# Turning the first layer's cached key pages in 32x32 blocks on VectorE, with the pages fetched by quarters of their width

## The chip, the cores and the metric

One core of one Trainium2 chip runs the whole program. The metric is the device time in microseconds (us) of one execution. The numbers of the trace come from one profiled execution, taken by the hardware profiler.

## The reference

Two layers of a hybrid decoder run as one step for two groups of requests: a prompt of 512 positions, and 8 samples of 8 new positions each that have 1024 cached positions behind them. The change is in the attention of layer 0, which has 8 forgetting ("fox") heads and 4 differential heads. For a sample it reads 8 cached pages of keys and 8 of values, each page 128 positions by 1024 floats:

```python
def fox_diff_attend(qa, qb, cq, q_pos, ka, va, ck, kb, vb, k_pos, lam, subln0):
    sa = jnp.einsum('bqhd,bkhd->bhqk', qa, ka).astype(jnp.float32) * scale
    sa = sa + (jnp.swapaxes(cq, 1, 2)[..., :, None] - jnp.swapaxes(ck, 1, 2)[..., None, :])
    pa = jax.nn.softmax(jnp.where(causal, sa, -jnp.inf), axis=-1)
    oa = jnp.einsum('bhqk,bkhd->bqhd', pa.astype(va.dtype), va)
    sb = jnp.einsum('bqhcd,bkhcd->bhcqk', qb, kb).astype(jnp.float32) * scale
    pb = jax.nn.softmax(jnp.where(causal, sb, -jnp.inf), axis=-1)
    diff = pb[:, :, 0] - lam * pb[:, :, 1]
    ob = jnp.einsum('bhqk,bkhe->bqhe', diff.astype(vb.dtype), vb)
...
        k_all = jnp.concatenate([cache_k[pt].reshape(past, L0_KV_WIDTH), k_b], axis=0)
        v_all = jnp.concatenate([cache_v[pt].reshape(past, L0_KV_WIDTH), v_b], axis=0)
```

The scores sum over the width of a key (the 64 columns of a head). TensorE sums over partitions, and a page lands with its positions on the partitions, so each key page has to be turned before it can be scored.

## The kernel before, in words

The class `FirstAttention` does the attention of layer 0 for the prompt and the samples in one stage. Its five methods `tensor`, `scalar`, `gpsimd`, `vector` and `sync` write out the order of TensorE (PE), ScalarE (ACT), GpSimd (POOL), VectorE (DVE) and SyncE (SP) by hand, with semaphores between them.

The stage has 32 slots. Slot x does one unit of the prompt, a pair of heads with one of the four query blocks of 128 rows: `PAIR_ORDER` takes the four differential pairs first (16 "mixed" units, whose two maps of probabilities are blended into one), then the four fox pairs. The query blocks come in the order 2, 1, 3, 0, so that a unit's width is 384, 256, 512 or 128 columns. Beside the prompt, slots 4b to 4b+3 (k = 0 to 3) carry sample b: its 8 key pages are turned, two in each slot, and scored from k = 1 on; the softmax comes at k = 0 of the next sample; its 8 value pages are weighed in the slots after that.

- **Loads.** SP issues one DMA for each page (`load_key` L1907, `load_value` L1912), of [128 partitions x 1024], 512 KB in rows of 4 KB. The page's number is first read into a register of SP (`value_load`, L1902), from which the address is worked out. There are 5 places for key pages, 4 for value pages and 3 for turned pages. A load into a used place waits until the page in it has been turned (`turned_b`) or weighed (`value_used`). Keys run 5 pages ahead. By the order of SP's loop, 52 of the 64 value pages are issued ahead of the last key page.
- **Turning.** `turn_keys` (L1468) makes 8 transposes of 128x128 for each page on PE (L1474), four into each of two PSUM banks (`RING`). ACT copies one bank to the turned page (`keys_out` L1621, copy at L1618), DVE the other (`keys_out` L1745, copy at L1749).
- **Scoring and weighing.** `score_page` (L1487, matmuls L1483) and `weigh_page` (L1521, matmuls L1531) use 32-wide tiles of PE; the prompt's scores, the transposes and the prompt's `weigh` use 128-wide or 64-wide tiles. A slot's order on PE is: scores, turn a page, weigh a page, turn the probabilities of unit x-1, score a page, turn a page, weigh a page, score a page, `weigh(x-1)`.
- **DVE** in a slot: the blend of unit x-1, the row maxima of unit x (`top`, L1762), one key copy, the second another, then the sums of unit x (L1767, L1771), and the samples' softmax pieces.

Of the kernel before, what the change touches and what calls it, by code (L numbers as in the profile page):

```python
# [18 lines left out]
P = 128  # L19
# [49 lines left out]
def constant_table():  # L69
# [13 lines left out]
    row_head, row_query = i // DEC_SEQ, i % DEC_SEQ  # L83
# [4 lines left out]
    put("selections", selections)  # L88
    put("new_mask", np.where(h8[None, :] <= row_query[:, None], 0.0, NEG))
# [1246 lines left out]
class FirstAttention:  # L1336
# [7 lines left out]
    def __init__(self, nc, K, mem, qp, kp, vp, qs, ks, vnew, retired, next_tile):  # L1344
# [3 lines left out]
                 "turned_a", "turned_b", "emptied_a", "emptied_b", "chain", "pool_chain",  # L1348
# [12 lines left out]
        self.knew, self.snew, self.st = sb("knew", [P, KC, DEC_SEQ]), sb("snew", [P, DEC_SEQ]), sb("st", [P, 2, 10])  # L1361
        self.squares = sb("squares", [P, DIFF, SEQ])
# [18 lines left out]
        self.fills_after_key = {}  # L1381
        self.fill_of_second_probs = {}
        self.fill_of_second_head = {}
# [21 lines left out]
    def tensor(self, pe):  # L1405
        K, S = self.K, self.S
        filled = [0, 0]
        turned, emptied = (S["turned_a"], S["turned_b"]), (S["emptied_a"], S["emptied_b"])

        def ring(x):  # L1410
            if filled[x]:
                pe.wait_ge(emptied[x], filled[x])
            filled[x] += 1
            return self.RING[x]
# [16 lines left out]
        def turn(u):  # L1431
            p, qt = self.units[u]
            for i in range(1 if self.mixed(u) else 2):
                bank = ring(i)
                if self.mixed(u):
                    pe.wait_ge(S["blended"], self.count(u + 1, True))
                for j in range(qt + 1):
                    ins = pe.transpose(bank[:, j * P:(j + 1) * P], self.probs[:, u % 2, i, j * P:(j + 1) * P], K.c("ident"))
                ins.then_inc(turned[i], 1)
                if i:  # L1440
                    self.fill_of_second_head[u] = filled[1]
            self.head_fills = (filled[0], filled[1])

        def weigh(u):
            p, qt = self.units[u]
            pe.wait_ge(emptied[0], self.head_fills[0])
            if not self.mixed(u):
                pe.wait_ge(emptied[1], self.head_fills[1])
# [1830 lines left out]
```

## Time and profile before

| | us |
|---|---|
| three runs | 1892.20, 1894.41, 1894.65 |
| median | 1894.41 |
| the profiled execution's own time | 1891.96 |
| its span, first to last instruction | 1890.2 |

The mean granted TensorE clock over the span is 0.957 of full. Over the span PE is busy 1707.6 us (90%), DVE 853.5 (45%), ACT 603.2 (32%) and POOL 151.1 (8%). The stage of the change runs from the first scores at 226.9 us to the first matmul of the next stage at 521.2 us.

How to read it: busy shares are means over stages that have different limits. Matmuls are pipelined, so that the time of a group of them is best read from one start to the next. DMA issues stand on the queue of the engine that issues them (SPq is SP's), and the time beside an issue is what SP spends on it; the transfer follows behind it. A DMA share near 1 says that the core's 16 DMA engines are all occupied.

### The profile page before, as it was taken

Reading aid. Unit: us, or ns where it says so; the run is one execution under the profiler, and the core shown is the slowest. Engines: PE = TensorE matmul, PEld = TensorE weight load, DVE = VectorE, ACT = ScalarE, POOL = GpSimd, SP = SyncE. Lnnn points to the kernel's source line nnn. Section 1 sums busy time; section 2 is a strip of 40 time slices with the busy share of each in tenths; the row PEclk is TensorE's granted clock in tenths of the full one; section 3 lists DMA queues with packets and bytes.
Section 4 is the critical chain, followed back from the end, with each engine's and each line's share of the span. In section 5 each row is a group of like instructions: output and inputs, shape, how many; then the busy total and the mean of one; then the engine's idle time right before and its main releaser. Section 6 shows DMA issues by size and latency. Waiting matters only on the chain. (4 is left out here: it accounts for less than half of the span.)

```text
span 1890.2 us, 32284 instructions
## 1 busy us (share of the span) xinstructions
PE 1707.6 (90%) x12454; PEld 1422.2 (75%) x12462; DVE 853.5 (45%) x1570; ACT 603.2 (32%) x1275; POOL 151.1 (8%) x303
## 2 busy tenths in 40 slices
PE   5999788998798999999998788687888999999998
PEld 3787565665478999799987576355457999889987
DVE  4446455445435322323224978985545232233323
ACT  3325344433223321112213344554333232112220
POOL 1222223111000000000000012110000000000000
PEclk9999899999898999999998899798999999999999
DMA  5232278766632222333321112101752322233221
GB/s 183 68 117 57 86 265 278 269 218 222 205 101 67 76 79 84 87 104 83 105 76 59 48 45 48 46 1 47 217 137 67 89 68 83 84 90 85 70 84 67
DMA packets 177043, 201.61 MB, mean 107 GB/s; under 512 B 21650, under 2 KB 131538, under 8 KB 176914
## 3 DMA queue, kind: packets, MB, share of 16 engines
q1 hardware_dynamic: 167634, 189.39, 32.6%
q10 hardware_dynamic: 9200, 10.24, 1.7%
q8 instruction: 81, 1.33, 0.3%
q14 instruction: 48, 0.39, 0.1%
q0 software_dynamic: 80, 0.26, 0.1%
HBM read 190.77 MB, written 9.08 MB: 106 GB/s over the span
## 5 line engine op out<-in xcount | busy, mean ns | idle before, releaser
L211 PE MATMUL ps<-feat_lo,w_hi 128*128 128x288 f32 x1408 | 416.5, 296 | 7.4 <-PEq L2451 3.8
L213 PE MATMUL ps<-feat_hi,w_hi 128*128 128x288 f32 x1408 | 416.5, 296 | 0.0
L212 PE MATMUL ps<-feat_hi,w_lo 128*128 128x288 f32 x1408 | 416.1, 296 | 0.0
L193 DVE TENSOR_TENSOR w_lo<-w_raw,w_hi 128x2048 fp32r<-128x2048 f32 x96 | 220.1, 2292 | 339.5 <-ACT w_hi L187 339.4
L187 ACT ACTIVATE w_hi<-w_raw 128x2048 fp32r<-128x2048 f32 x96 | 183.6, 1913 | 348.8 <-PE ps L219 334.9
L211 PEld LDWEIGHTS ps<-feat_lo,w_hi 128*128 128x128 f32 x1408 | 265.7, 189 | 8.6 <-issue 4.4
L212 PEld LDWEIGHTS ps<-feat_hi,w_lo 128*128 128x128 f32 x1408 | 265.7, 189 | 0.0
L213 PEld LDWEIGHTS ps<-feat_hi,w_hi 128*128 128x128 f32 x1408 | 265.5, 189 | 0.0
L2551 DVE TENSOR_TENSOR f_prod<-f_silu,ps 128x576 f32<-128x576 f32 x44 | 33.2, 754 | 361.1 <-ACT f_silu L2530 361.1
L211 PE MATMUL ps<-w_lo,feat_hi 128*128 128x512 f32 (+1 forms) x448 | 182.4, 407 | 13.5 <-DVE feat_lo L2403 5.5
L212 PE MATMUL ps<-w_hi,feat_lo 128*128 128x512 f32 (+1 forms) x448 | 177.9, 397 | 0.0
L213 PE MATMUL ps<-w_hi,feat_hi 128*128 128x512 f32 (+1 forms) x448 | 177.8, 397 | 0.0
L2530 ACT ACTIVATE f_silu<-ps 128x576 f32<-128x576 f32 x44 | 28.7, 652 | 429.6 <-PE ps L213 429.6
L212 PE MATMUL ps<-w_hi,f_act_lo 128*128 128x512 f32 x352 | 137.0, 389 | 0.0
L211 PE MATMUL ps<-w_lo,f_act_hi 128*128 128x512 f32 x352 | 137.0, 389 | 0.0
L213 PE MATMUL ps<-w_hi,f_act_hi 128*128 128x512 f32 x352 | 136.9, 389 | 0.0
L211 PEld LDWEIGHTS ps<-w_lo,feat_hi 128*128 128x128 f32 x448 | 88.6, 198 | 32.3 <-issue 14.4
L213 PEld LDWEIGHTS ps<-w_hi,feat_hi 128*128 128x128 f32 x448 | 87.9, 196 | 17.9
L212 PEld LDWEIGHTS ps<-w_hi,feat_lo 128*128 128x128 f32 x448 | 88.6, 198 | 16.1
L1474 PE MATMUL ps<-const,places 128*128 128x128 f32 x512 | 70.7, 283 | 13.4 <-ACT a_probs_t L1618 8.6
L213 PEld LDWEIGHTS ps<-w_hi,f_act_hi 128*128 128x128 f32 x352 | 66.1, 188 | 13.7
L211 PEld LDWEIGHTS ps<-w_lo,f_act_hi 128*128 128x128 f32 x352 | 66.1, 188 | 13.6
(340 smaller groups left out, 2386.4 us busy)
## 6 DMA issues: line engine op xcount, KB each, us to landing
places<-in_cache_l_k_dram SPq DMA_DIRECT2D x64, 512.0 KB, 4.5
places<-in_cache_l_v_dram SPq DMA_DIRECT2D x64, 512.0 KB, 5.1
w_raw<-in_w_gate_dram SPq DMA_DIRECT2D x44, 512.0 KB, 4.0
w_raw<-in_w_up_dram SPq DMA_DIRECT2D x44, 512.0 KB, 5.3
w_raw<-in_w_in_dram SPq DMA_DIRECT2D x18, 1024.0 KB, 5.2
w_raw<-in_w_down_dram SPq DMA_DIRECT2D x16, 1024.0 KB, 5.1
s_kslot<-in_cache_l_k_dram SPq DMA_DIRECT2D x56, 128.0 KB, 2.8
w_raw<-in_w_down_dram SPq DMA_DIRECT2D x8, 768.0 KB, 4.3
```

The lines of the kernel that those rows point to most:

```text
L187: act.activation(self.K.w_hi[:, n % 2, :], self.K.w_raw[:, n % 2, :], ACT.Copy).then_inc(self.split_hi, 1)
L193: dve.tensor_tensor(self.K.w_lo[:, n % 2, :], self.K.w_raw[:, n % 2, :], self.K.w_hi[:, n % 2, :].bitcast(F32), ALU.subtract).then_inc(sel ...
L211: pe.matmul(out, lhs[0], rhs[1], start=start, stop=False)
L212: pe.matmul(out, lhs[1], rhs[0], start=False, stop=False)
L213: return pe.matmul(out, lhs[0], rhs[0], start=False, stop=stop)
L1474: ins = pe.transpose(bank[:, c * P:(c + 1) * P], self.keys[g % self.KEY_PLACES][:, at:at + P], K.c("ident"))
L2530: act.activation(silu[:, x, :, :], K.ps[:, 4 * x:4 * x + 2, 0:H], ACT.Silu).then_inc(S["silu_ok"], 1)
L2551: dve.tensor_tensor(prod[:, x, :, :], silu[:, x, :, :], K.ps[:, 4 * x + 2:4 * x + 4, 0:H], ALU.mult)\
```

## The change

A key page is no longer turned by PE. SP fetches it by quarters of its width: four DMAs for each page, quarter a (256 columns) into partitions 32a to 32a+31, each of those partitions holding four runs of 256 columns, 1 KB each. So the block structure of the turned page is made by the DMAs, and what is left is a transpose of each 32x32 block, which one VectorE instruction does for the whole page from SBUF to SBUF. The order of the rows of a turned page is another one than before; the queries (`q_rows`), the samples' new keys (`k_rows`), the table `selections`, and the copies out of the samples' probabilities are reordered to suit, and a small matmul by the constant `swap` reorders the softmax factor.

```diff
@@ FirstAttention.tensor
-        def turn_keys(g):
-            pe.wait_ge(self.k_in[g % self.KEY_PLACES], 16 * (g // self.KEY_PLACES + 1))
-            for x in range(2):
-                bank = ring(x)
-                for c in range(4):
-                    at = (4 * x + c) * P
-                    ins = pe.transpose(bank[:, c * P:(c + 1) * P], self.keys[g % self.KEY_PLACES][:, at:at + P], K.c("ident"))
-                ins.then_inc(turned[x], 1)
...
-            pe.wait_ge(emptied[0], self.key_fills[g][0])
-            pe.wait_ge(emptied[1], self.key_fills[g][1])
+            pe.wait_ge(S["keys_turned"], g + 1)
...
         for x in range(self.SLOTS + 1):
             b, k = divmod(x, 4)
-            if k == 1 and b >= 2:
+            if k == 1 and b:
+                turn_new_probs(b - 1)
+                swap_factor(b - 1)
+            if k == 2 and b >= 2:
                 turn_o(b - 2)
             if x < self.SLOTS:
                 scores(x)
-                turn_keys(2 * x)
+            if x:
+                turn(x - 1)
...
             if before >= 0:
                 weigh_page(before, first)
-            if x:
-                turn(x - 1)
-            if x < self.SLOTS and k:
-                score_page(b, 2 * k - 2)
-            if x < self.SLOTS:
-                turn_keys(2 * x + 1)
-            if before >= 0:
                 weigh_page(before, first + 1)
...
             if x < self.SLOTS and k:
+                score_page(b, 2 * k - 2)
                 score_page(b, 2 * k - 1)
@@ FirstAttention.scalar
-        def keys_out(g):
-            if g >= self.TURNED_PLACES:
-                act.wait_ge(S["page_scored"], g - self.TURNED_PLACES + 1)
-            empty(self.turned[g % self.TURNED_PLACES][:, 0:4, :], self.RING[0].rearrange("p (c n) -> p c n", n=P))
...
         def head_out(u):
-            if u >= 2:
-                act.wait_ge(S["weighed"], u - 1)
-            empty(self.probs_t[:, u % 2, 0, 0:self.width(u)], self.RING[0][:, 0:self.width(u)])
+            for i in range(1 if self.mixed(u) else 2):
+                if i == 0 and u >= 2:
+                    act.wait_ge(S["weighed"], u - 1)
+                empty(self.probs_t[:, u % 2, i, 0:self.width(u)], self.RING[i][:, 0:self.width(u)])
...
+        def probs_out(b):
+            nonlocal emptied
+            for half in range(2):
+                dst = self.pt[:, 4 * half:4 * half + 4, :].rearrange("p j (x y q) -> p y (j x) q", x=4, y=4)
+                src = self.RING[half].rearrange("p (j y x q) -> p y j x q", j=4, y=4, x=4)
+                emptied += 1
+                act.wait_ge(S["act_turned"], emptied)
+                for y in range(4):
+                    ins = act.activation(dst[:, y].rearrange("p (j x) q -> p j x q", j=4), src[:, y], ACT.Copy)
+                ins.then_inc(S["act_emptied"], 1)
@@ FirstAttention.vector
-        def keys_out(g):
+        def turn_keys(g):
+            dve.wait_ge(self.k_in[g % self.KEY_PLACES], 64 * (g // self.KEY_PLACES + 1))
             if g >= self.TURNED_PLACES:
                 dve.wait_ge(S["page_scored"], g - self.TURNED_PLACES + 1)
-            bank = filled()
-            dve.tensor_copy(self.turned[g % self.TURNED_PLACES][:, 4:8, :], bank.rearrange("p (c n) -> p c n", n=P))\
-               .then_inc(S["emptied_b"], 1)
+            src = self.keys[g % self.KEY_PLACES].rearrange("p (g c n) -> p g c n", g=4, c=KC)
+            dst = self.turned[g % self.TURNED_PLACES].rearrange("p c (g n) -> p g c n", g=4)
+            dve.transpose(dst, src).then_inc(S["keys_turned"], 1)
@@ FirstAttention.sync
         def load_key(g):
             if g >= self.KEY_PLACES:
-                sp.wait_ge(S["turned_b"], self.fills_after_key[g - self.KEY_PLACES])
-            sp.dma_start(self.keys[g % self.KEY_PLACES], page(K.cache_l0_k, g)).then_inc(self.k_in[g % self.KEY_PLACES], 16)
+                sp.wait_ge(S["keys_turned"], g - self.KEY_PLACES + 1)
+            src = page(K.cache_l0_k, g).rearrange("(g k) (a n) -> a k g n", g=4, a=4)
+            dst = self.keys[g % self.KEY_PLACES].rearrange("p (g n) -> p g n", g=4)
+            for a in range(4):
+                sp.dma_start(dst[32 * a:32 * a + 32], src[a]).then_inc(self.k_in[g % self.KEY_PLACES], 16)
```

Besides, GpSimd copies a sample's queries with 4 instructions instead of 16, ACT empties the banks that held both halves of the samples' probabilities, and DVE no longer copies a second head of probabilities.

The order of SP, one key page and one value page, with what it waits for. Before (`places` are the key and value buffers; `a0_turned_b` says that a key page has left its place):

```order
L1902 TENSOR_LOAD pages [waits a0_turned_b]
L1902 ISA x2
L1910 ISA
L1910 DMA places<-in_cache_l_k_dram 128x1024
L1902 TENSOR_LOAD pages [waits a0_value_used]
L1902 ISA x2
L1922 ISA
L1922 DMA places<-in_cache_l_v_dram 128x1024
```

After, one key page:

```order
L1921 TENSOR_LOAD pages [waits a0_keys_turned]
L1921 ISA x2
L1932 ISA
L1932 DMA places<-in_cache_l_k_dram 32x4x256
L1932 ISA
L1932 DMA places<-in_cache_l_k_dram 32x4x256
L1932 ISA
L1932 DMA places<-in_cache_l_k_dram 32x4x256
L1932 ISA
L1932 DMA places<-in_cache_l_k_dram 32x4x256
```

The address instruction and the DMA stand four times behind one page number, and the DMA has 32 partitions of 4 runs of 256 elements. The value page keeps its form.

The order of PE in one slot of the mixed units (the third slot of a sample, of width 512). Before:

```order
L1423 MATMUL ps<-kp,qp 128x512 x2
L1428 MATMUL ps<-causal_bf,ident_bf 128x128 x2
L1474 MATMUL ps<-const,places 128x128 x8
L1531 MATMUL ps<-places,free_49 32x256 x4
L1438 MATMUL ps<-const,a_probs 128x128 x2
L1483 MATMUL ps<-places,free_49 32x128 x8
L1474 MATMUL ps<-const,places 128x128 x8
L1531 MATMUL ps<-places,free_49 32x256 x4
L1483 MATMUL ps<-places,free_49 32x128 x8
L1464 MATMUL ps<-a_probs_t,vp 128x128 x2
```

After:

```order
L1424 MATMUL ps<-kp,qp 128x512 x2
L1429 MATMUL ps<-causal_bf,ident_bf 128x128 x2
L1441 MATMUL ps<-const,a_probs 128x128 x2
L1528 MATMUL ps<-places,free_49 32x256 x8
L1471 MATMUL ps<-places,free_49 32x128 x16
L1463 MATMUL ps<-a_probs_t,vp 128x128 x2
```

The 16 transposes of key pages are gone, the turn of the probabilities stands right behind the scores, and the two weighings and the two scorings stand together.

The order of DVE in the same kind of slot, with what it waits for. Before:

```order
L1762 TENSOR_REDUCE a_minus<-ps 128x2 [waits a0_scored]
L1749 COPY places<-ps 128x512 [waits a0_turned_b,a0_page_scored] x2
L1767 RECIPROCAL a_scale<-a_total 128x2 [waits a0_exped]
L1771 TENSOR_SCALAR a_scale<-a_scale,minus_lam 128x1 [waits a0_summed]
L1777 SCALAR_TENSOR_TENSOR a_probs<-a_probs,a_scale 128x256 [waits a0_chain,a0_scaled]
```

After:

```order
L1783 TENSOR_REDUCE a_minus<-ps 128x2 [waits a0_scored]
L1779 STREAM_TRANSPOSE places<-places 128x4x8x32 [waits a0_page_scored,a0_k_in_0]
L1779 STREAM_TRANSPOSE places<-places 128x4x8x32 [waits a0_page_scored,a0_k_in_1]
L1788 RECIPROCAL a_scale<-a_total 128x2 [waits a0_exped]
L1792 TENSOR_SCALAR a_scale<-a_scale,minus_lam 128x1 [waits a0_summed]
```

Two transposes that wait for the pages' DMAs (`a0_k_in_0`, `a0_k_in_1`) stand where two copies out of PSUM waited for PE.

## Rows read from the trace of the kernel before

**Rows 1.** Windows: us; busy us (x instructions) per engine; PEclk, DMA share, GB/s.
```profile
226.00:493.50 267.50, 241.58 (x2835) 162.76 (x2836) 127.93 (x305) 108.25 (x307) 55.10 (x162) 0.97 0.72 241
342.00:346.00 4.00, 4.00 (x50) 2.55 (x52) 2.39 (x5) 2.49 (x7) 0.00 (x0) 1.00 0.98 377
700.00:701.00 1.00, 1.00 (x10) 1.00 (x9) 0.00 (x0) 0.00 (x0) 0.00 (x0) 1.00 1.05 410
1141.00:1142.00 1.00, 1.00 (x5) 0.51 (x3) 0.97 (x4) 1.00 (x6) 0.00 (x0) 1.00 1.07 229
```

**Rows 2.** Timeline of SPq (SP's DMA queue) in the stage: start us, us, operation, xcount.
```profile
229.38 5.28 SPq L1910 DMA_DIRECT2D places<-in_cache_l_k_dram  x5
234.71 0.43 SPq L1927 DMA_DIRECT2D bias_raw<-fox_rows  x1
...
232.15 2.52 SPq L1910 DMA_DIRECT2D places<-in_cache_l_k_dram  x3
...
475.96 0.33 SPq L1910 DMA_DIRECT2D places<-in_cache_l_k_dram  x1
476.33 0.38 SPq L1933 DMA_DIRECT2D vs<-out_s_l_v_dram  x1
```

**Rows 3.** Waits of SP, 226 to 515 us: us in total, times, longest us.
```profile
SPq L1902 <- PE ps L1474: 111.3, 56, 8.1
...
SPq L1902 <- PE ps L1531: 16.5, 7, 3.8
```

**Rows 4.** Timeline of PE: the last key pages' scores and the next stage's first matmul.
```profile
496.40 1.08 PE L1483 MATMUL ps<-places,free 128*32 128x128 f32 x32
...
521.22 0.77 PE L211 MATMUL ps<-w_lo,feat_hi 128*128 128x512 f32 x1 [3.17 <-DVE feat_lo L2403]
```

**Rows 5.** Timeline of SPq: issues of other shapes, elsewhere in the kernel.
```profile
1316.66 3.99 SPq L2027 DMA_DIRECT2D s_kslot<-in_cache_l_k_dram  x8
...
1154.67 1.26 SPq L180 DMA_DIRECT2D w_raw<-in_w_out_dram  x2
...
1300.75 0.50 SPq L2687 DMA_DIRECT2D mask_rows<-sample_mask  x1
...
1886.84 0.54 SPq L2923 DMA_DIRECT2D out_y_sample_dram<-resid  x1
```

**Rows 6.** Page, part 6: KB of each DMA, median us from issue to landing.
```profile
s_kslot<-in_cache_l_k_dram SPq DMA_DIRECT2D x56, 128.0 KB, 2.8
```

**Rows 7.** Groups by line and form, 226 to 493.5 us: busy us, mean ns | idle before.
```profile
L1474 PE MATMUL ps<-const,places 128*128 128x128 f32 x511 | 70.6, 283 | 13.4 <-ACT a_probs_t L1618 8.6 <-DMA places<-in_cache_l_k_dram 4.6
...
L1749 DVE COPY places<-ps 128x512 f32<-128x512 f32 x63 | 43.4, 688 | 61.3 <-PE ps L1474 61.3
L1762 DVE TENSOR_REDUCE a_minus<-ps 128x2 f32<-128x1024 f32 x8 | 9.8, 1225 | 7.9 <-PE ps L1428 7.9
...
L1618 ACT ACTIVATE places<-ps 128x512 f32<-128x512 f32 x64 | 38.4, 600 | 92.3 <-PE ps L1474 92.3
```

**Rows 8.** Page, part 5: VectorE's largest group of two operands.
```profile
L193 DVE TENSOR_TENSOR w_lo<-w_raw,w_hi 128x2048 fp32r<-128x2048 f32 x96 | 220.1, 2292 | 339.5 <-ACT w_hi L187 339.4
```

**Rows 9.** Timeline of PE within one slot.
```profile
274.88 0.64 PE L1531 MATMUL ps<-places,free 128*32 128x256 f32 x8
275.45 0.44 PE L1438 MATMUL ps<-const,a_probs 128*128 128x128 f32 x2
275.82 0.65 PE L1483 MATMUL ps<-places,free 128*32 128x128 f32 x16
276.51 1.06 PE L1474 MATMUL ps<-const,places 128*128 128x128 f32 x8
```

**Rows 10.** Windows as in rows 1: two neighbouring stretches of the stage.
```profile
411.00:418.00 7.00, 7.00 (x43) 5.98 (x46) 1.20 (x5) 0.87 (x2) 2.92 (x1) 0.51 0.26 97
418.00:425.00 7.00, 7.00 (x134) 5.19 (x126) 2.98 (x7) 2.17 (x7) 0.00 (x0) 1.00 0.65 225
```

More of the change, by code:

```diff
@@ L1406, in tensor, with ring @@
         K, S = self.K, self.S
[L1407 to L1413, printed above, removed]
+        fills = {"act": 0, "dve": 0}
+        holder = [None, None]
+        def ring(x, who):
+            if holder[x] is not None:
+                pe.wait_ge(S[holder[x][0] + "_emptied"], holder[x][1])
+            fills[who] += 1
+            holder[x] = (who, fills[who])
             return self.RING[x]
@@ L1515, in turn_probs, with turn_new_probs, swap_factor @@
                                        K.c("ident"))
-                ins.then_inc(turned[half], 1)
-            self.probs_fills[b] = (filled[0], filled[1])
-            pe.transpose(ring(1)[0:DEC_SEQ, 0:P], self.s_probs[:, PAST_LEN:KEYS], K.c("ident")).then_inc(turned[1], 1)
-            self.fill_of_second_probs[b] = filled[1]
+                ins.then_inc(S["act_turned"], 1)
+            self.probs_fills[b] = fills["act"]
+        def turn_new_probs(b):
+            bank = ring(0, "act")
+            pe.wait_ge(S["s_exped"], 3 * b + 3)
+            pe.transpose(bank[0:DEC_SEQ, 0:P], self.s_probs[:, PAST_LEN:KEYS], K.c("ident")).then_inc(S["act_turned"], 1)
+            self.new_fills[b] = fills["act"]
+        def swap_factor(b):
+            bank = ring(1, "dve")
+            pe.wait_ge(S["weighted"], b + 1)
+            pe.matmul(bank[:, 0:1], K.c("swap"), self.st[:, b % 2, 9:10], start=True, stop=True).then_inc(S["dve_turned"], 1)
         def weigh_page(b, j):
@@ L1667, in scalar @@
                 exps(x)
-                keys_out(2 * x + 1)
+            if k == 0 and b:
+                sample_exps(b - 1)
             if self.SQUARES <= x < self.SQUARES + DIFF:
@@ L1683, in gpsimd, with spread_keys @@
             pool.sem_clear(range(lo, hi))
+        def spread_keys():
+            for a in range(4):
+                for half in range(2):
+                    for x in range(2):
+                        at = HEAD_DIM * half + 32 * x
+                        s.ok(pool.tensor_copy(self.k_rows[32 * a:32 * a + 32, 2 * half + x::4, :],
+                                              self.ks[at:at + 32, 2 * a:2 * a + 2, :]))
+                        s.wait()
+            pool.sem_inc(S["k_spread"], 1)
         def queries(b):
@@ L1691, in queries @@
                 pool.wait_ge(S["bias_ok"], b + 1)
-            s.ok(pool.tensor_copy(self.knew[:, :, :], self.ks[:, :, b * DEC_SEQ:(b + 1) * DEC_SEQ]))
-            flat = self.qz[:, :, :].rearrange("p c n -> p (c n)")
-            for half in range(2):
-                rows = slice(half * HEAD_DIM, (half + 1) * HEAD_DIM)
-                for c in range(KC):
-                    col = c * P + 16 * c + 8 * half
-                    s.wait()
-                    ins = s.ok(pool.tensor_copy(flat[rows, col:col + DEC_SEQ], self.qs[rows, c, b * DEC_SEQ:(b + 1) * DEC_SEQ]))
-            s.wait()
+            for a in range(4):
+                rows = slice(32 * a, 32 * a + 32)
+                at = DEC_SEQ * a
+                dst = K.free0[rows, at:at + 4 * 288].rearrange("p (i r) -> p i r", r=288)[:, :, 0:2 * P]\
+                    .rearrange("p i (x n) -> p i x n", x=2)[:, :, :, 0:DEC_SEQ]
+                src = self.q_rows[rows, :, b * DEC_SEQ:(b + 1) * DEC_SEQ].rearrange("p (i x) n -> p i x n", x=2)
+                s.ok(pool.tensor_copy(dst, src))
+                s.wait()
             pool.sem_inc(S["q_ok"], 1)
@@ L1857, in vector @@
                 shift(b - 1)
+            if k == 1 and b:
+                factor_out(b - 1)
             if x:
                 blend(x - 1)
-            if k == 1 and b >= 2:
+            if k == 2 and b >= 2:
                 o_finish(b - 2)
@@ L1884, in vector @@
                 sums(x)
-            if k == 0 and b:
-                sample_probs_out(b - 1)
+        factor_out(LAST)
         finish(self.SLOTS - 1)
```

137 lines of the change are left out of this document (69 added, 68 removed).

## The prediction

> **What bounds the kernel now.** I read the busy times by window first, for the change touches one stage only. From 226 to 493.5 us PE is busy 241.58 of 267.50 us, DVE 127.93, ACT 108.25, and the DMA share is 0.72 at 241 GB/s [rows 1]. So PE is the bound of this stage, and the DMA engines are not far behind: in single stretches, as at 342 us, their share is 0.98 at 377 GB/s. The page's shares over the whole span would hide both.
>
> Next I read SP's queue, because the change makes SP issue four DMAs where it issued one. SP issues the first key page at 229.38 and the last at 475.96 us, 246.6 us apart [rows 2]. In the waits it stands 111.3 us for PE's key transposes (L1474) and 16.5 us for the weighing (L1531) [rows 3], part of the latter after the last key. The rest is its own work. Three key pages in a row take 2.52 us, the last counted to the end of its 0.33 us DMA [rows 2]: (2.52 - 0.33) / 2 = 1.095 us a page, of which 0.33 is the DMA instruction and 0.765 the page number and the address. A value page has the same four rows in the order, so the same price. Up to the last key page there are 64 key pages and 52 value pages, 116 x 1.095 = 127.0 us, and 8 biases at 0.43 and 7 rows of new values at 0.38 [rows 2], 6.1 us. That is 133.1 us of work, and with 111.3 of waits 244.4 of the 246.6 us: the account closes. **SP has about 111 us to spare in this stage, and no more.**
>
> **The change, part by part.**
>
> *TensorE.* 512 transposes go, eight in a row starting 1.06 us or a little less before the next group [rows 9, 7]: 64 x 1.03 = some 66 us of PE time. The regrouping also saves switches between tile widths: a weighed page takes 0.57 us from its start to the start of a 128-wide group behind it, 274.88 to 275.45, and its eight records cover only 0.64 [rows 9]; some four such switches fewer in each of 32 slots, at an estimated 0.2 us, give about 25 us. What is left is 241.6 - 66 - 25 = 150 us, 4.7 us a slot, beside a pitch of 8.3 now. If nothing else bound the stage it would be much shorter.
>
> *VectorE.* 64 copies of 0.688 us go (43.4 us for 63) [rows 7], 64 transposes of 128x1024 elements come. No transpose of this engine is in the trace. Its nearest row is a reduction over as many elements, 1.225 us [rows 7]; half of the operation over 128x2048 with two operands, 2.292 us [rows 8], gives 1.15; the far end is that it costs as much as that whole row, 2.29. I take 1.2: 77 us, so that DVE has 127.9 - 43.4 + 77 = 162 us of work, and even at 2.29 some 231. The stage's 270 or more hide it.
>
> *ScalarE* loses 64 copies of 0.600 us [rows 7] and takes over smaller copies; it waits 92.3 us for those transposes today, so it is covered either way. GpSimd's fewer copies lie beside other work, too. I cost both at nothing; PE's own work is the cover.
>
> *SyncE.* This is the term that decides. Each key page adds three address instructions and three DMAs, and its one DMA of 128 partitions becomes four of 32 partitions with four 1 KB runs. The step from one DMA to the next with one address instruction between them is in the trace: eight pieces of `s_kslot` take 3.99 us to the end of the last one's 0.33 [rows 5], a pitch of 0.523, so 0.19 beside the DMA itself. With d for the new DMA instruction a key page costs 0.765 + 3 x 0.19 + 4d = 1.335 + 4d. What d is no row shows. DMAs of 128 partitions take 0.33 [rows 2, 5], one of 16 partitions (the bias, in one run a partition) 0.43 [rows 2], those of 64 partitions in one run 0.50 and 0.54, and the 64-partition tile of four 2 KB runs 1.26 / 2 = 0.63 [rows 5]. It is not the bytes that make them dearer, but a count of partitions other than 128. The ends are 0.33 (even 0.37 would be near it) and 0.63. I take 0.53, halfway between the 16-partition row and the 64-partition row in four runs, since the quarter has 32 partitions in four runs.
>
> SP's work up to the last quarter is then 133.1 + 64 x (3 x 0.19 + 4d - 0.33) = 133.1 + 15.4 + 256d = 148.5 + 256d; at d = 0.53, 284.2 us. That is more than the 246.6 us of today, waits included: the waits are used up, SP is the bound, and the five places no longer fill ahead. The last quarter is issued by 229.4 + 284.2 = 513.6 us. Then 2.8 us for landing (a DMA of 128 KB [rows 6]), 1.2 for the transpose and 0.6 for the last page's score (half of the 1.08 us group [rows 4]): 518.2 us. Today the last scores end at 496.40 + 1.08 = 497.5. What follows them, up to the next stage at 521.22 [rows 4], the softmax and eight value pages of the last sample, stays: its transfers wait for places just as now. **The shift is 518.2 - 497.5 = +20.7 us**, or as a formula 256d - 115. It is zero at d = 0.45, +46 at 0.63, and -31 at 0.33.
>
> *The transfers.* A quarter writes 32 partitions. The tiles that write 64 partitions move 229 GB/s at a DMA share of 1.07, those of 128 partitions 410 [rows 1]. At 229 GB/s a key page of 512 KB takes 2.29 us, and a value page at 377 GB/s 1.39: 64 x 2.29 + 52 x 1.39 = 219 us up to the last key, less than 284. Hidden behind SP, at that rate.
>
> The sum against the profiled execution: 1891.96 + 20.7 = 1912.7. The median of the three runs, 1894.41, stands 2.45 higher, so I expect **1915 us**. Forecast: slower.
>
> **The rivals.**
>
> *A, the issue is as short as that of 128 partitions (faster).* At d = 0.33 to 0.37 the formula gives -31 to -20. The transfers' 219 us and PE's 150 lie below SP's 233 to 243, so that SP still paces the stage, but faster than PE does now. Some -25: 1869 us. It decides below d = 0.45. For it: the quarter has 128 runs, as many as a whole page has now. Against it: all three rows with 64 partitions lie at 0.50 or above [rows 5]. The Trainium skill, "DMA: Bandwidth & Descriptors", section "Issuing engines are not separate DMA queues", says that the sequencer's time to start a DMA is usually small relative to the DMA itself. By that rule SP would not be the bound and case A, or better, would come. The trace speaks against it: a key page's issue is 1.095 us of SP's time beside some 1.39 us of data at 377 GB/s, so it is not small here even before the change.
>
> *B, writing 32 partitions halves the rate again.* 410 GB/s at 128 partitions and 229 at 64 [rows 1] could go on to about 115 at 32. A key page would take 4.6 us, the 64 with 52 value pages 64 x 4.6 + 52 x 1.39 = 367 us, the last key would land near 229.4 + 367 + 2 = 598 and the shift be about +100: 1995 us. It decides once a key page's data take over 3.3 us, (284 - 72) / 64. Against it: consecutive quarters go to different partitions, and several are in flight. The Trainium skill, "SBUF — State Buffer", section "Door 1: The DMA port swizzle", has 32 and 64 partitions of such a block reach the same number of ports; by it the rate would not fall below that of 64 partitions, and no run here shows it yet.
>
> *C, the transpose costs 2.29 us.* Under my forecast it is hidden. Under A two of them in a slot of 7.5 us, with the row maxima and the blend before and between them, would take back most of the gain: about -5.
>
> *D, the clock.* In one stretch of this stage the granted clock was 0.51, and PE did 43 matmuls in 7 us where it does 134 at full [rows 10]. PE will idle nearly half of a slot of 8.9 us. Where the clock is at the lower level, 4.7 us of work becomes 9.4, more than the slot. Ten such slots would add some 5 us to any of the cases.
>
> **How the numbers follow.** SP binds with d from 0.46 to 0.65: 0.55. A, with C as its poorer part: 0.34. B: 0.04. D beside a d near break-even: 0.02. The remaining 0.05 is d close to 0.45. The faster side is 0.34, the slower 0.61, and within 0.2% of the time before (3.8 us, about what a measurement of this kernel can tell from no change) 0.05. The likeliest case alone spans 1899 to 1941. The range reaches from A at d = 0.33, 1864, to SP at d = 0.63, 1941; it leaves out B and what lies between the transfers' bound and A.
>
> **What would show it.** In the profile after: the DMA issues of the key pages on SP at 0.5 us or more each, four to a page; SP's wait for turned keys gone or nearly; DVE's transposes waiting for the key DMAs, with PE waiting for DVE; the stage's PE share down to some 55%; the transposes at about 1.2 us. If SP's waits for `keys_turned` remain in tens of us, SP is not the bound and my step on d is wrong. If the key DMAs land ever later after their issue, with the DMA share near 1, B is right.

## The result, and the profile after the change

The change makes the kernel slower, as forecast, by a little less than forecast:

| | us |
|---|---|
| before, median of 5 runs | 1893.42 (1891.92 to 1894.65) |
| after, median of 5 runs | 1907.71 (1896.78 to 1910.06) |
| ratio | 1.0064, 95% interval 1.0037 to 1.0092 |
| forecast | 1915, range 1864 to 1941 |
| the profiled execution after, own time | 1896.78 |

The profiled execution is the fastest of those of the changed kernel, and they scatter more than before. Its stage is only some 6 us longer than before, where the median of the runs is 14 us longer. I read from its trace where things wait, and take the sizes from the comparisons of runs.

The stage's windows after the change, with the columns of [rows 1]:

```profile
226.00:501.00 275.00, 216.44 (x2382) 133.87 (x2380) 146.52 (x284) 90.29 (x329) 41.50 (x74) 0.78 0.97 234
260.00:460.00 200.00, 161.96 (x1715) 99.70 (x1706) 104.55 (x212) 62.44 (x235) 27.68 (x43) 0.79 1.01 234
231.00:240.00 9.00, 1.55 (x6) 0.64 (x6) 2.75 (x4) 2.12 (x5) 7.28 (x21) 0.50 0.65 195
```

VectorE's group of transposes, with the columns of [rows 7]:

```profile
L1779 DVE STREAM_TRANSPOSE places<-places 128x1024 f32<-128x1024 f32 x64 | 78.0, 1232 | 56.4 <-PE ps L1471 50.3 <-DMA places<-in_cache_l_k_dram 6.1
```

PE is busy 216 us of 275, at a granted clock of 0.78 against 0.97 in [rows 1]. The DMA share went from 0.72 to 0.97, while the bytes for each us fell from 241 to 234 GB/s. VectorE's transpose takes 1.232 us, the price that I had taken; it waits 50.3 us for PE to score pages and only 6.1 for the key DMAs.

SP's queue in the timeline, as in [rows 2]: the first pages, some of the middle, and the last key page.

```profile
227.97 12.62 SPq L1932 DMA_DIRECT2D places<-in_cache_l_k_dram  x20
...
229.47 0.32 SPq L1932 DMA_DIRECT2D places<-in_cache_l_k_dram  x1
...
231.08 9.52 SPq L1932 DMA_DIRECT2D places<-in_cache_l_k_dram  x16
...
231.08 1.82 SPq L1932 DMA_DIRECT2D places<-in_cache_l_k_dram  x4
...
302.49 1.82 SPq L1932 DMA_DIRECT2D places<-in_cache_l_k_dram  x4
...
306.18 2.38 SPq L1932 DMA_DIRECT2D places<-in_cache_l_k_dram  x4
...
486.74 1.85 SPq L1932 DMA_DIRECT2D places<-in_cache_l_k_dram  x4
```

A quarter's DMA instruction takes 0.32 us. Four quarters in a row take 1.82 us, and four pages 9.52, so a key page costs SP (9.52 - 1.82) / 3 = 2.57 us; now and then four quarters take longer, as the 2.38 at 306 us. My formula 1.335 + 4d with d = 0.32 gives 2.61. The last key quarter is issued by 486.74 + 1.85 = 488.6, 12.3 us later than the last key page of [rows 2].

The turning of the last page, its scores and the next stage's first matmul, the latter two as in [rows 4]:

```profile
500.17 1.25 DVE L1779 STREAM_TRANSPOSE places<-places 128x1024 f32<-128x1024 f32 x1 [0.94 <-PE ps L1471]
...
502.08 1.08 PE L1471 MATMUL ps<-places,free 128*32 128x128 f32 x32
...
526.86 0.77 PE L212 MATMUL ps<-w_lo,feat_hi 128*128 128x512 f32 x1 [3.17 <-DVE feat_lo L2425]
```

The last scores end at 503.2 us, 14.6 us behind the last quarter's issue and not the 4.6 that I had reckoned: VectorE could not turn the last page when it landed, but waited for PE to score an earlier one (the releaser in the first line), and PE scores pages in the order of its slots. From the last scores to the next stage it is 23.7 us, as it was before (521.22 - 497.5).

The waits of SP and of PE for loads, where SP stood 111.3 us in [rows 3]:

Waits of SP from 226 to 495 us (us in total, times, longest; this stretch for all waits below where no other is named):

```profile
SPq L1921 <- DVE places L1779: 19.6, 11, 6.2
SPq L1921 <- PE ps L1528: 2.8, 4, 2.2
```

Waits of PE in its stage (us in total, times, longest):

```profile
PE ps L1528 <- DMA places<-in_cache_l_v_dram: 22.3, 12, 3.7
PE ps L1441 <- DVE a_probs L1798: 16.6, 11, 6.3
```

PE's wait for value pages before, up to 515 us; all of it lies behind 495 us:

```profile
PE ps L1531 <- DMA places<-in_cache_l_v_dram: 6.4, 4, 3.3
```

One such wait in the timeline after the change, and VectorE's transpose behind it:

```profile
484.83 1.08 PE L1528 MATMUL ps<-places,free 128*32 128x256 f32 x8 [3.16 <-DMA places<-in_cache_l_v_dram]
...
487.79 1.25 DVE L1779 STREAM_TRANSPOSE places<-places 128x1024 f32<-128x1024 f32 x1 [5.46 <-PE ps L1471]
```

Part 6 of the page (KB of each DMA, median us from issue to landing):

```profile
places<-in_cache_l_k_dram SPq DMA_DIRECT2D x256, 128.0 KB, 4.6
places<-in_cache_l_v_dram SPq DMA_DIRECT2D x64, 512.0 KB, 7.0
```

The value pages in part 6 of the page before:

```profile
places<-in_cache_l_v_dram SPq DMA_DIRECT2D x64, 512.0 KB, 5.1
```

SP's wait for turned keys fell from 111.3 to 19.6 us; PE now stands 22.3 us for value pages in a stretch in which it never did before. While it stands it scores no key page, so that no place for a turned page comes free and VectorE stands too: here 5.46 us, with most of PE's 3.16 in them. A value page takes 7.0 us from its issue to its landing, 5.1 before. From the first to the last key quarter it is 260.6 us. Work at 133.1 + 64 x (2.57 - 1.095) = 227.5 us and the 19.6 of waits (most of the 2.8 lie behind the last quarter) fill 247 of them; longer DMA instructions are a good part of the rest. SP is nearly full, but it is not the only one that is.

### The profile page after: what moved, and what is told of

It reads as the page before. It is cut to its first block and busy times, and to the rows that moved or that the text cites. A ratio compares the mean times of both kernels' runs of the same rounds, so it can differ in the third digit from the quotient of the medians.

```text
span 1895.0 us, 31580 instructions
## 1 busy us (share of the span) xinstructions
PE 1680.2 (89%) x11958; PEld 1391.0 (73%) x11966; DVE 870.6 (46%) x1546; ACT 586.6 (31%) x1307; POOL 137.7 (7%) x215
## 5 line engine op out<-in xcount | busy, mean ns | idle before, releaser
L1779 DVE STREAM_TRANSPOSE places<-places 128x1024 f32<-128x1024 f32 x64 | 78.0, 1232 | 56.4 <-PE ps L1471 50.3
```

The lines of the kernel that those rows point to most:

```text
L1779: dve.transpose(dst, src).then_inc(S["keys_turned"], 1)
```

## The experiments

The trace left several causes open: SP's issues (S), transfers into 32 partitions at a time (T), the clock (C) and the new order on PE (O). Twelve kernels were run.

| kernel | median us | ratio to before, 95% interval |
|---|---|---|
| the change | 1907.7 | 1.0064 (1.0037 to 1.0092) |
| one DMA for each key page | 1865.8 | 0.9838 (0.982 to 0.9856) |
| four quarters of all 128 partitions | 1883.4 | 0.9931 (0.9914 to 0.9948) |
| one DMA, SP slowed | 1895.7 | 1.0012 (0.9997 to 1.0027) |
| quarters by rows (32 partitions, 4 KB) | 1901.4 | 1.0042 (1.0025 to 1.006) |
| extra PE work | 1909.1 | 1.0073 (1.0049 to 1.0098) |
| old order in a slot | 1907.4 | 1.0056 (1.0039 to 1.0073) |
| quarters in the order 0, 2, 1, 3 | 1900.0 | 1.0034 (1.0009 to 1.0058) |
| quarters from two queues | 1893.0 | 0.9998 (0.9981 to 1.0014) |
| half of the pages turned by PE | 1911.1 | 1.0096 (1.0079 to 1.0113) |
| all pages turned by PE | 1974.9 | 1.0421 (1.0402 to 1.044) |
| values on ACT's queue, 0, 1, 2, 3 | 1885.1 | 0.9952 (0.9933 to 0.9971) |
| values on ACT's queue, 0, 2, 1, 3 | 1874.1 | 0.9886 (0.9866 to 0.9905) |

### One DMA for each key page

```diff
-            for a in range(4):
-                sp.dma_start(dst[32 * a:32 * a + 32], src[a]).then_inc(self.k_in[g % self.KEY_PLACES], 16)
+            sp.dma_start(self.keys[g % self.KEY_PLACES], page(K.cache_l0_k, g)).then_inc(self.k_in[g % self.KEY_PLACES], 64)
```

> The changed kernel with each key page fetched by one DMA of 128 partitions in 4 KB rows, as before the change; the transposes on VectorE and all else stay. The turned pages then hold other keys and columns than the scores assume, so the samples' attention of layer 0 is computed on permuted keys; the number of instructions elsewhere is unchanged. Theory T (writing 32 partitions at a time fills the DMA engines): the DMA share of the stage falls from 0.97 to about 0.7, values land at about 5 us instead of 7.0, the time falls by some 25 to 45 us, to 1865 to 1885. Theory S (SP's four issues for each page): SP's work falls by 64 x 1.5 = 96 us; the same fall of the time, so this run alone does not part T from S. Theory C (PE idles, its clock falls, and that alone costs the time): the clock of the stage stays at 0.78 or less and the time within 8 us of the changed kernel. Theory O (the new order of PE is at fault): no change within 8 us.

1865.8 us: 42.0 us less than the changed kernel, 28.6 less than before. It turns the pages into another order than the scores need, so it serves to measure with and can't be used. So the rest of the change, transposes on VectorE and PE relieved, is worth some 29 us, and the fetch by quarters takes 42. C and O, which had this run stay within 8 us, are out as sole causes; the stage's clock hardly rose (0.84 against 0.79 in the window below).

Of the run with one DMA for each key page:

Its windows (columns as in [rows 1]):

```profile
260.00:460.00 200.00, 176.25 (x2045) 110.51 (x2044) 120.27 (x241) 73.26 (x278) 29.59 (x49) 0.84 0.78 262
```

Waits of SP in its stage (us in total, times, longest):

```profile
SPq L1921 <- DVE places L1779: 77.0, 37, 4.8
```

Waits of PE for value pages:

```profile
PE ps L1528 <- DMA places<-in_cache_l_v_dram: 7.0, 4, 3.8
```

### Four quarters of all 128 partitions

```diff
-                sp.dma_start(dst[32 * a:32 * a + 32], src[a]).then_inc(...)
+                sp.dma_start(self.keys[g % self.KEY_PLACES][:, cols], src[:, cols]).then_inc(...)
```

Here `cols` is `slice(256 * a, 256 * a + 256)` and `src` the whole page.

> The changed kernel with four DMAs for each key page, each of 128 partitions by 256 columns: as many DMAs, as many 1 KB runs and bytes, but each writes all partitions. As above the samples' keys are permuted. Theory T: as fast as the run with one DMA for each page, within 8 us, with a DMA share near 0.7 to 0.8 in the stage. Theory S: as slow as the changed kernel, 1897 to 1910, since SP issues as much. C and O: no change within 8 us. If 1 KB runs are what costs, not the partitions, the share stays near 0.97 and the time does not fall.

1883.4 us, between the two: neither T alone nor S alone. Against one DMA, 17.6 us come back with four issues and 1 KB runs; against the change, 24.3 us go where every DMA writes all partitions.

Of the run with wide quarters:

Its windows (columns as in [rows 1]):

```profile
260.00:460.00 200.00, 167.47 (x1962) 103.21 (x1961) 116.33 (x231) 68.75 (x257) 29.59 (x48) 0.85 0.83 255
```

SP in its timeline (start us, us):

```profile
228.99 1.35 SPq L1932 DMA_DIRECT2D places<-in_cache_l_k_dram  x2
...
472.02 1.91 SPq L1932 DMA_DIRECT2D places<-in_cache_l_k_dram  x4
```

Waits of SP in its stage (us in total, times, longest):

```profile
SPq L1921 <- PE ps L1528: 7.7, 10, 4.0
...
SPq L1921 <- DVE places L1779: 0.6, 2, 0.4
```

The last page's scores:

```profile
484.98 1.08 PE L1471 MATMUL ps<-places,free 128*32 128x128 f32 x32
```

Part 6 of its page:

```profile
places<-in_cache_l_k_dram SPq DMA_DIRECT2D x256, 128.0 KB, 3.1
places<-in_cache_l_v_dram SPq DMA_DIRECT2D x64, 512.0 KB, 4.4
```

SP waits 0.6 us for turned keys where it waited 77.0 with one DMA, so here SP paces the stage. In the middle of the stage the DMA share is 0.83 at 255 GB/s; the change has 1.01 at 234 in the same window. The same 128 KB land in 3.1 us instead of 4.6, a value page in 4.4 instead of 7.0.

### One DMA, with SP slowed

```diff
+            for _ in range(3):
+                number(g)
             sp.dma_start(self.keys[g % self.KEY_PLACES], page(K.cache_l0_k, g)).then_inc(self.k_in[g % self.KEY_PLACES], 64)
```

> The run with one DMA of 128 partitions for each key page (the samples' keys permuted), with three more reads of the page number in front of each key DMA: SP spends about as much on a key page as on four quarters, but the transfers are those of one DMA. If SP's own work is what holds back the run with four wide quarters: about its 1883 us, plus or minus 5, and SP's waits for turned keys near 0. If its 1 KB runs on the DMA engines are: near the 1866 us of the run with one DMA.

1895.7 us, 29.9 us more than without the three reads, at the same transfers. That SP's own time is enough to set the end is shown. The figure is 12 us above the expected 1883, since SP was slowed by more than the quarters slow it:

Of the run with SP slowed:

SP in its timeline (start us, us):

```profile
228.35 0.46 SPq L1931 DMA_DIRECT2D places<-in_cache_l_k_dram  x1
...
476.38 0.39 SPq L1931 DMA_DIRECT2D places<-in_cache_l_k_dram  x1
...
480.51 0.39 SPq L1931 DMA_DIRECT2D places<-in_cache_l_k_dram  x1
...
484.64 0.39 SPq L1931 DMA_DIRECT2D places<-in_cache_l_k_dram  x1
```

Waits of SP in its stage (us in total, times, longest):

```profile
SPq L1921 <- DVE places L1779: 1.3, 5, 0.4
```

Waits of PE for value pages, and these pages in part 6:

```profile
PE ps L1528 <- DMA places<-in_cache_l_v_dram: 22.6, 12, 4.5
...
places<-in_cache_l_v_dram SPq DMA_DIRECT2D x64, 512.0 KB, 4.7
```

A key page comes every 4.13 us (480.51 to 484.64, a value page between), with 1.3 us of waits for turned keys in the whole stage. From the first key page to the end of the last one's issue it is 484.64 + 0.39 - 228.35 = 256.7 us here and 472.02 + 1.91 - 228.99 = 244.9 with the wide quarters: 11.8 us of SP, 12.3 us between the medians and 8.3 between the two profiled executions. If the 1 KB runs of the wide quarters cost something of their own, the times would lie closer together than SP's work; by the medians they do not, by the profiled executions by 3.5 us. So the 1 KB runs cost a few us at most.

The run also shows how a full queue of SP reaches PE. PE stands 22.6 us for value pages, as much as in the changed kernel (22.3) and three times as much as without the three reads (7.0), though the pages' median landing is 4.7 us. They come late because SP issues them late.

### Quarters by rows, and quarters in another order

```diff
-                sp.dma_start(dst[32 * a:32 * a + 32], src[a]).then_inc(...)
+                sp.dma_start(self.keys[g % self.KEY_PLACES][32 * a:32 * a + 32], src[32 * a:32 * a + 32]).then_inc(...)
```

(`src` is the whole page), and, for itself:

```diff
-            for a in range(4):
+            for a in (0, 2, 1, 3):
```

> Four DMAs for each key page, each of 32 partitions by 1024 columns, in rows of 4 KB: as the changed kernel in issues and partitions, other than it only in the run length (the samples' keys are permuted). If writing 32 partitions at a time is the cost: as the changed kernel, 1900 to 1910, DMA share near 0.97. If it is the 1 KB runs in that form: between 1880 and 1890.

> The changed kernel, whole, with the quarters issued in the order 0, 2, 1, 3, so that neighbours in a queue write different halves of the partitions. If neighbouring DMAs overlap on a DMA engine enough for the halves to be written side by side: 5 to 25 us faster than the changed kernel. If each is written out before the next: within 5 us.

Rows of 4 KB into 32 partitions: 1901.4 us, as the change within the intervals (1.0025 to 1.006 against 1.0037 to 1.0092), not near 1885. The window from 260 to 460 us of the run with rows of 4 KB:

```profile
260.00:460.00 200.00, 161.57 (x1735) 98.83 (x1736) 105.78 (x212) 64.49 (x240) 26.71 (x43) 0.79 0.99 235
```

The DMA share and the rate are close to those of the change, too (1.01 and 234). So at least 18.0 of the 24.3 us (1901.4 less 1883.4) hang on the 32 partitions, and what is left for the run length is not clear of noise. The order 0, 2, 1, 3 gives 1900.0, and its interval overlaps with that of the change too: by itself it settles nothing.

### Extra work on PE, and the old order in a slot

```diff
+                if i == 0:
+                    for j in range(12):
+                        pe.transpose(bank[:, j % 4 * P:(j % 4 + 1) * P], K.c("ident"), K.c("ident"))
```

This stands in `turn`, ahead of the wait for the blended probabilities. The other kernel puts `turn(x - 1)` back between the two `weigh_page` and `score_page(b, 2 * k - 2)` behind it.

> The changed kernel with 12 extra transposes of a constant in each slot, put ahead of PE's wait for the blended probabilities, into a bank that the true transposes overwrite: some 1.5 us of PE work a slot, mostly where PE would wait. Theory C: the stage's mean clock rises from 0.78 towards 0.95 and the time falls by 5 to 15 us. T and S: the DMA share stays at 0.97 and the time stays within 5 us, or rises by up to 15 us where the extra work is in the way.

> The changed kernel with PE's order in a slot as before the change (weigh a page, turn the probabilities, score a page, weigh a page, score a page), without the grouping by tile kind; everything else of the change stays. Theory O: faster by 5 us or more. T, S and C: within 5 us, or slower by up to 10 us for the switches between tile widths that come back, 2 in each slot.

The window of the stage with the extra work:

```profile
226.00:501.00 275.00, 232.75 (x2657) 162.03 (x2657) 143.25 (x278) 86.86 (x323) 41.43 (x74) 0.87 0.99 229
```

The clock rose from 0.78 to 0.87 and the time did not fall (1909.1): the lower clock accompanies the loss and is not what causes it, with the reservation that the 12 transposes cost PE something themselves. The run with one DMA says the same: it is 28.6 us faster than before at a clock of 0.84. The old order gives 1907.4, the change 1907.7: the grouping of the tile kinds is worth nothing that the runs can tell while SP and the transfers bind.

### Quarters from two queues

```diff
-            for a in range(4):
+            for a in range(2):
                 sp.dma_start(dst[32 * a:32 * a + 32], src[a]).then_inc(self.k_in[g % self.KEY_PLACES], 16)
@@ FirstAttention.scalar
+            load_key(2 * x + self.KEY_PLACES)
+            load_key(2 * x + self.KEY_PLACES + 1)
```

ACT's `load_key` reads the page number itself and issues quarters 2 and 3.

> The changed kernel, whole, with quarters 0 and 1 of each key page issued by SP and quarters 2 and 3 by ACT at the end of its slot. SP's work on a key page falls from 2.6 to about 1.6 us, and writes to the lower and the upper 64 partitions are in flight side by side. If both SP and the transfers bind and the two halves do not share a limit: some 20 to 40 us faster than the changed kernel, 1868 to 1888. If the limit on the transfers is one of the engines as a whole: the share stays near 0.97 and the time within 8 us of 1907. If ACT's extra work, some 100 us, gets in the way of its exponentials: slower than the changed kernel.

1893.0, 14.7 us less than the change and equal to before: less of a gain than 1868 to 1888, more than the 8 us of the second case, so that none of the three cases came as stated. SP has time again (80.4 us of waits for turned keys), but the share stays high and the rate low:

Of the run with two queues:

Its windows (columns as in [rows 1]):

```profile
260.00:460.00 200.00, 171.50 (x1802) 105.63 (x1801) 108.44 (x216) 66.24 (x242) 28.03 (x44) 0.77 0.94 234
```

Waits of SP in its stage (us in total, times, longest):

```profile
SPq L1936 <- DVE places L1794: 80.4, 34, 4.9
```

That writing the lower and upper halves from two queues would lift the rate was not borne out (234 GB/s in this window, as in the change). How much ACT's 128 issues cost its exponentials was not parted from that.

### Half of the pages, and all of them, turned by PE

```diff
+                for c in range(4):
+                    for a in range(4):
+                        at = 256 * a + 32 * (4 * x + c)
+                        ins = pe.matmul(bank[self.rows4[a], c * P:(c + 1) * P], src[:, at:at + 32], K.c("ident"),
+                                        start=True, stop=True)
```

These matmuls stand behind `turn(x - 1)`, for every second page in the one kernel and for all pages in the other; such pages come by one DMA, and ACT and DVE copy half a page each.

> The changed kernel, whole, but every second key page is fetched by one DMA of 128 partitions and turned on PE, by 32 matmuls of 32 columns with the identity (tiles as wide as those of scoring and weighing, so that no switch is added), into the same order of rows as VectorE's transposes give; ACT and DVE copy half a page each out of PSUM. SP's work falls by 32 x 1.5 = 48 us, half of the writes of 32 partitions go, PE gains about 32 x 1.3 = 42 us. If SP's issues and the 32-partition writes are what cost the change its gain: half of the 42 us between the changed kernel and the run with one DMA come back and the rest is room, so 1875 to 1890, faster than both. If PE binds again: near 1894.

> As the run with every second page, but all key pages: none is turned by VectorE and each is fetched by one DMA. What is left of the change is the order of PE with the tile kinds grouped, the rows' order, and the copies moved to ACT. If the grouping alone is worth something: 1880 to 1892. If PE's work, with 64 x 1.3 = 83 us of turning, binds as before the change: 1890 to 1900. If VectorE's transposes were the gain that the fetch hides: slower than the run with every second page by 10 us or more.

1911.1 and 1974.9: the first misses its ranges. The second is over 10 us slower than the first, which was to tell that VectorE's transposes were the gain, but it can't be read so, as turning by PE cost more than I had reckoned. Two pages take 3.90 us of PE in the second kernel, in its timeline, not the 2 x 1.3 = 2.6 of the expectation:

```profile
337.04 3.90 PE L1439 MATMUL ps<-const,places 128*32 128x128 f32 x128 [0.63 <-ACT a_probs_t L1647]
```

And in the first PE stands 15.6 us in all, up to 500 us, until ACT has emptied a bank:

```profile
PE ps L1439 <- ACT a_probs_t L1647: 15.6, 28, 0.8
```

They don't say what the grouping alone is worth, as their turning is dearer than that of before. That PE is the bound again in them is argued from their PE waits and the price of the turning; it was not tried by itself.

### Value pages on ACT's queue

```diff
@@ FirstAttention.sync
-                if self.VALUE_PLACES <= h < G:
-                    load_value(h)
@@ FirstAttention.scalar
             if k == 0 and b:
                 probs_out(b - 1)
+            for half in range(2):
+                if x < 2:
+                    load_value(2 * x + half)
+                if self.VALUE_PLACES <= 2 * x - 6 + half:
+                    load_value(2 * x - 6 + half)
```

Run with the quarters in the order 0, 2, 1, 3, and then in 0, 1, 2, 3.

> The changed kernel, whole, with SP issuing only key quarters (in the order 0, 2, 1, 3) and ACT issuing the value pages at the end of its slots. SP's work on a pair of pages falls from 3.7 to 2.6 us, ACT's rises by 64 x 1.1 = 70 us. A value page no longer stands behind four quarters in one queue. If SP's issues are what binds together with the 32-partition writes: faster than the changed kernel by 15 to 35 us, 1870 to 1890, with SP now waiting for turned keys. If the transfers alone bind: within 5 us of the 1900 us of the run with that order of quarters, with the DMA share near 0.97. If ACT gets in the way: slower than that.

> The changed kernel, whole, with the value pages issued by ACT and the key quarters by SP in the order 0, 1, 2, 3: other than the changed kernel in the queue of the values alone. If taking SP's work for the values away is what gives the gain of the run with both: 1868 to 1880, within 6 us of that run. If the order of the quarters gives a good part, as the run with that order alone let one think (1900 for 1908): 1880 to 1890.

With the order of the change, 1885.1 us: 22.7 less than the change for nothing but the queue of the value pages and the point of their issue. With 0, 2, 1, 3 it is 1874.1, another 11.0 less, and here the intervals are apart (0.9866 to 0.9905 against 0.9933 to 0.9971). The second one beats both kernels: 19 us below before, 34 below the change. The first expectation came true (1870 to 1890, with SP waiting for turned keys). Of the second one the case came in which the order gives a good part (1880 to 1890): the queue gives two thirds, the order one third.

Of the run with 0, 2, 1, 3:

Its windows (columns as in [rows 1]):

```profile
260.00:460.00 200.00, 172.97 (x2039) 109.13 (x2038) 121.04 (x243) 73.80 (x275) 30.18 (x49) 0.85 1.01 259
```

Waits of SP in its stage (us in total, times, longest):

```profile
SPq L1943 <- DVE places L1801: 44.2, 28, 4.6
```

Waits of PE in its stage (us in total, times, longest):

```profile
PE ps L1528 <- DMA places<-in_cache_l_v_dram: 6.9, 7, 2.1
```

Its group of transposes on VectorE:

```profile
L1801 DVE STREAM_TRANSPOSE places<-places 128x1024 f32<-128x1024 f32 x64 | 78.1, 1233 | 45.3 <-PE ps L1471 25.8 <-DMA places<-in_cache_l_k_dram 19.5
```

And of the run with 0, 1, 2, 3 the same window, the transposes, PE's waits and the value pages in part 6:

```profile
260.00:460.00 200.00, 172.52 (x2008) 109.16 (x2000) 117.42 (x235) 69.20 (x255) 30.25 (x49) 0.83 1.04 252
...
L1801 DVE STREAM_TRANSPOSE places<-places 128x1024 f32<-128x1024 f32 x64 | 78.4, 1235 | 57.2 <-DMA places<-in_cache_l_k_dram 29.1 <-PE ps L1471 28.1
...
PE ps L1528 <- DMA places<-in_cache_l_v_dram: 5.2, 5, 2.1
...
places<-in_cache_l_v_dram ACTq DMA_DIRECT2D x64, 512.0 KB, 9.2
```

With 0, 1, 2, 3 a value page takes 9.2 us from its issue to its landing, longer than the 7.0 of the change, but it is issued without standing behind four quarters, and PE's wait for values falls from 22.3 to 5.2 us. Now it is the key quarters that come late: VectorE waits 29.1 us for them, where it was 6.1 in the change. The order 0, 2, 1, 3 brings this to 19.5, 9.6 us less, beside the 11.0 us of the time. Moving the values changes two things at once, SP's work and the queue in which the values stand; these runs do not part the two. The DMA share stays near 1 and the rate rises from 234 to 252 and 259 GB/s: the share alone had not been a limit.

## Why the prediction was right, and where its steps failed

- **SP's queue takes up its spare time and then sets the end: right in part.** Its waits for the keys fell from 111.3 us [rows 3] to 19.6, and the slowed SP costs 29.9 us at equal transfers. Taking the value pages off SP gives 22.7 us back, with the reservation above. But in the changed kernel SP is not the only limit. My own sign that it is not, waits for `keys_turned` left in tens of us, is nearly met by the 19.6; they are 0.6 and 1.3 in the two runs where SP alone sets the pace. The Trainium skill, "DMA: Bandwidth & Descriptors", section "Issuing engines are not separate DMA queues", has the time to initiate a DMA as usually small relative to the DMA itself. Here it was not: 2.57 us a key page on SP, and the end moved with it.
- **d = 0.53: the mis-sized term.** It measured 0.32, below even the lower end of 0.33 that I had kept. The 64-partition rows at 0.50 to 0.63 [rows 5] were no guide for 32 partitions, and "a count of partitions other than 128" is not what makes an issue dearer. At 0.32 my formula gives 256 x 0.32 - 115 = -33 us, a gain.
- **What the formula left out.** With quarters 128 partitions wide, where SP paces alone, the runs give 1883.4 against 1894.3, a gain of 10.9 us where the formula has some 30: it is about 20 us too low there. The traces show two terms that I had too small. From the first to the last quarter SP takes 244.9 us with the wide quarters, where the formula has 233 (d = 0.33), and 260.6 in the changed kernel, where it has 230 (d = 0.32); there 19.6 are waits for turned keys, which I had put at nothing. And the last scores do not follow 4.6 us behind the last quarter, but 12.1 us with the wide quarters (484.98 + 1.08 - 473.93) and 14.6 in the changed kernel, since PE and the three places for turned pages stand between. The next stage follows the last scores as I had said.
- **"Hidden behind SP": the step on the transfers that failed.** I set 219 us of transfers against 284 of SP's work and took the larger. Writing 32 partitions at a time raises a quarter's landing from 3.1 to 4.6 us and a value page's from 4.4 to 7.0, and costs 24.3 us where I had zero. Why the two don't hide each other is argued: with no time to spare on SP no load can be issued early enough to make up for a longer landing. For it speaks that with the values on ACT's queue they land later still (9.2 us) and PE waits less for them, though VectorE then waits longer for the quarters (29.1 us).
- **The path.** I had late key quarters hold VectorE, and VectorE hold PE. VectorE waited only 6.1 us for key quarters, and 50.3 for PE. What came late were the value pages behind the quarters on SP's queue: PE stood 22.3 us for them, and its share of the stage was 79%, not some 55%.
- **Luck in the number.** d was some 54 us too dear, the transfers 24 too cheap, and about 20 us stood in no term (the bullet above on the formula). These errors have opposite signs, and what is left of them is the difference between the forecast +20.7 and the measured +14.3. The direction was right for a reason partly other than the one that I gave.
- **Rival A** had its condition met (d below 0.45), and its gain did not come, because it rested on the same "transfers below SP" and the same formula. **Rival B** is out in its strong form (at the stage's 234 GB/s, keys and values together, 512 KB take 2.24 us, not 4.6), but its direction, a price for narrow writes, was right. **C** is out: 1.232 us. **D**: the clock did fall, to 0.78; raising it to 0.87 with extra work gave nothing.
- **PE's work** of 150 us measured 216 busy, at the lower clock; extra work on it changed the time by no more than the scatter (1909.1). No run shows the 25 us of saved switches in it by themselves: the old order made no difference, but PE did not bind there. VectorE was hidden as costed.

## What to carry to other kernels

Before cutting a load into several DMAs, add up what the issuing queue spends on the whole stage, address work included, and set it against that queue's waits in the trace; what it waits is all there is to spend. Look also at what else stands in that queue: here the value pages behind the quarters came late, not the quarters. Then don't take the larger of issue time and transfer time for the cost, since a queue without time to spare may not issue early enough to cover a longer landing. The remedy that worked with the quarters as they are was giving the other stream of loads to another engine's queue, and ordering neighbours so that they write different parts of the partitions.

## What the runs showed of the hardware that was not expected

- The DMA instruction of a [32 partitions x 4 x 1 KB] quarter took 0.32 us on SP, less than the 0.50 to 0.63 of the 64-partition forms in [rows 5].
- DMAs of 32 partitions drove the DMA share to 1.01 at 234 GB/s where those of 128 partitions, with the same 1 KB runs, stood at 0.83 with 255 GB/s. A share near 1 was no limit: with the values on another queue it was 1.01 at 259 GB/s.
- Alternating the quarters between partitions 0 to 63 and 64 to 127 was worth 11.0 us once SP had time to spare. The Trainium skill, "SBUF — State Buffer", section "Door 1: The DMA port swizzle", places these halves on different ports. The gain is what that would lead one to expect; no run here shows the ports themselves, and from two queues the halves gained no rate.
- In the first stretch of the stage, with key quarters alone, the queue moved 195 GB/s at a share of 0.65: SP's pace, not the transfers', sets that stretch.
